# Own buffers for two weight sums, nine low parts of a step on GpSimd, and another order of the up-projection's units

## The reference, cut to what matters

```
up  = rms_norm(x) @ w_up                    # 1024 -> 2 x 2816, 576 tokens
upc = causal_dwconv(up, buf, cw, cb)        # width 3, per feature
val, gate = split(upc)
x   = x + (gelu(gate) * val) @ w_down       # 2816 -> 1024
```

## Time and profile before

| | us |
|---|---|
| median of 3 runs (lowest, highest) | 1084.98 (1084.79, 1086.69) |
| profiled execution, its own time | 1084.38 |
| its span | 1082.2 |
| busy PE, DVE, ACT, POOL | 1023.0, 788.7, 515.6, 425.6 |
| granted TensorE clock, mean | 0.988 |

### The profile page before, as it was taken

The page is one execution under the profiler, slowest core; times in us unless marked ns, Lnnn a source line. Parts: engine busy times, 40 slices in busy tenths (PEclk is TensorE's granted clock), DMA queues, the critical chain, the costliest instruction groups (busy, mean ns, idle before and its releaser), DMA issues.

```text
span 1082.2 us, 19980 instructions
## 1 busy us (share of the span) xinstructions
PE 1023.0 (95%) x7688; PEld 993.2 (92%) x7688; DVE 788.7 (73%) x1280; ACT 515.6 (48%) x935; POOL 425.6 (39%) x276
## 2 busy tenths in 40 slices
PE   8999999999999999999999868889999999999996
PEld 7899999999999999999999867889999999999885
DVE  6786558947576465674545778999999999999954
ACT  7666886223343443433323455544454444445553
POOL 4333443432223222232243425455555545455530
PEclk9999999999999999999999989999999999999998
DMA  8533322666696885946524112333232323223047
GB/s 208 167 101 102 83 79 82 147 191 159 140 259 140 225 215 140 246 110 212 179 80 117 40 39 79 98 92 85 69 105 62 108 70 104 73 76 101 25 101 206
DMA packets 263267, 132.94 MB, mean 123 GB/s; under 512 B 82720, under 2 KB 257045, under 8 KB 262920
## 3 DMA queue, kind: packets, MB, share of 16 engines
q1 hardware_dynamic: 262966, 131.63, 44.6%
q10 hardware_dynamic: 210, 0.07, 0.0%
HBM read 104.17 MB, written 25.29 MB: 120 GB/s over the span
## 4 chain that ended last, share of the span: by engine, by line
PE 57%; DVE 18%; issue 14%; POOL 5%; ACT 3%; DMA 2%; SPq 0%; DVEq 0%; ACTq 0%; POOLq 0%
PE ring L2667 38%; PE bank L3058 4%; PE ring L3072 4%; POOL f_lo L1211 4%; DVE val_taps L1813 3%; DVE f_stage L2398 3%; PE bank L2909 2%; PE ring L3058 2%; POOL wlo L1168 2%; DVE bank L1813 1%; ACT f_hi L1605 1%; DVE f_lo L2479 1%; PE bank L2713 1%; DVE f_stage L2405 1%; DMA d_stage<-in_w_down 1%
## 5 line engine op out<-in xcount | busy, mean ns | idle before, releaser
L1168 POOL TENSOR_TENSOR wlo<-stage,whi 128x1024 fp32r<-128x1024 f32 x78 | 199.0, 2552 | 401.8 <-ACT whi L1224 401.8
L2667 PE MATMUL ring<-x_split,whi 128*128 128x322 f32 (+2 forms) x1952 | 347.5, 300 | 0.0
L2667 PEld LDWEIGHTS ring<-x_split,whi 128*128 128x128 f32 x1952 | 294.4, 189 | 8.9 <-issue 8.1
L1211 POOL TENSOR_TENSOR f_lo<-f_stage,f_hi 128x512 fp32r<-128x512 f32 x110 | 155.1, 1428 | 195.7 <-ACT f_hi L1605 195.6
L2667 PE MATMUL ring<-x_split,wlo 128*128 128x256 f32 (+1 forms) x976 | 210.4, 297 | 0.0
L2667 PEld LDWEIGHTS ring<-x_split,wlo 128*128 128x128 f32 x976 | 164.6, 189 | 0.0
L1224 ACT ACTIVATE whi<-stage 128x1024 fp32r<-128x1024 f32 x79 | 83.3, 1054 | 80.6 <-PE ring L2667 70.6
L1605 ACT ACTIVATE f_hi<-f_stage 128x512 fp32r<-128x512 f32 x154 | 90.4, 627 | 22.8 <-DVE f_stage L2391 11.9
L3058 PE MATMUL bank<-fx_T,f_hi 128*128 128x290 f32 x264 | 79.5, 301 | 8.3 <-ACT sum_two L1688 5.1
L3058 PE MATMUL bank<-fx_T_lo,f_hi 128*128 128x290 f32 x264 | 78.5, 297 | 0.0
L3058 PE MATMUL bank<-fx_T,f_lo 128*128 128x290 f32 x264 | 78.4, 297 | 0.0
(11 more groups left out here) (425 smaller groups left out, 2361.1 us busy)
## 6 DMA issues: line engine op xcount, KB each, us to landing
stage<-in_w_in SPq DMA_DIRECT2D x56, 512.0 KB, 4.2
f_stage<-in_w_up SPq DMA_DIRECT2D x44, 512.0 KB, 5.1
d_stage<-in_w_down SPq DMA_DIRECT2D x40, 256.0 KB, 2.7
stage<-in_w_branch_a SPq DMA_DIRECT2D x8, 512.0 KB, 3.7
c_sample<-in_state_mlstm_C SPq DMA_DIRECT2D x16, 256.0 KB, 6.3
out_s_mlstm_C<-c_sample SPq DMA_DIRECT2D x16, 256.0 KB, 2.4
stage<-in_w_branch_b SPq DMA_DIRECT2D x8, 512.0 KB, 3.8
stage<-in_w_out SPq DMA_DIRECT2D x8, 512.0 KB, 3.7
```

What stands on the lines that cost most here:

```text
L1168: pool.tensor_tensor(spaced(wlo[:, slot]), packed(stage[:, slot, 0:n]), spaced(whi[:, slot]).bitcast(F32), ALU.subtract).then_inc(w_lo, 1)
L1211: pool.tensor_tensor(in_blocks(flo[n % RING], key), packed(piece(key)), in_blocks(fhi[n % RING], key).bitcast(F32), ALU.subtract).then_inc ...
L2667: last = pe.matmul(of(z, t0 or -2, t1), w[:, kk * WS:kk * WS + P], x_, start=kk == 0 and m == 0, stop=kk == kn - 1 and m == 2)
```

## The change

T2 and T4 get one buffer each, `weight_sum_T2` and `weight_sum_T4`, where the SBUF layout had 5888 unused bytes (step 0 keeps the old places). All nine low parts of a step (seven units and two D; seven in a step without D) are GpSimd's. TensorE's order in a step becomes B11, T4', D, T1, B21, T2, D, B22, T3 in place of B11, T1, D, T4', T2, B21, B22, D, T3. VectorE and ScalarE get new orders, and the semaphore counts come from lists of these orders (`sum_order` with C21 of the step before, C11, C22, C12; `weight_sum_order`; `copy_order`; `tap_order`).

```diff
@@ -215,16 +215,16 @@
     for i in range(NPAIR):
         d = down_at(i)
         yield "B11", i
-        yield "T1", i
+        if i:
+            yield "T4", i - 1
         if d:
             yield "D", *d
-        if i:
-            yield "T4", i - 1
+        yield "T1", i
+        yield "B21", i
         yield "T2", i
-        yield "B21", i
-        yield "B22", i
         if d:
             yield "D", d[0], d[1] + 1
+        yield "B22", i
         yield "T3", i
     g0, g1 = GROUPS - 2, GROUPS - 1
     yield "D", g0, 0
@@ -242,8 +242,7 @@
 UNIT = {key: n for n, key in enumerate(PIECES)}
 DOWN = tuple(key for key in PIECES if key[0] == "D")
 DOWN_AT = {key: n for n, key in enumerate(DOWN)}
-QUARTER = {"B11": 0, "B21": 1, "T1": 2, "B22": 3, "T3": 4, "T2": 0, "T4": 1}
-SUM_AT = {"T3": 1, "T1": 2, "T2": 3, "T4": 4}
+QUARTER = {"B11": 0, "B21": 1, "T1": 2, "B22": 3, "T3": 4}
 X_FIRST = {"B11": 1, "T3": 2}
 X_LATER = {"B21": 1, "T1": 2, "T2": 3, "T4": 4, "B22": 5}
 
@@ -268,7 +267,7 @@
     return UNIT[key] + 1
 
 
-SPLIT_BY_DVE = ("B22", "T3")
+SPLIT_BY_DVE = ()
 SPLIT_AT = {key: n + 1 for n, key in enumerate(key for key in PIECES if key[0] not in SPLIT_BY_DVE)}
 SPLIT_AT.update({key: n + 1 for n, key in enumerate(key for key in PIECES if key[0] in SPLIT_BY_DVE)})
 
@@ -288,19 +287,67 @@
     return T_FFN + n
 
 
-def parts(i, n):
-
-    return 3 * i + n
-
-
-def added(i, block):
-
-    return 3 * i + {"C11": 1, "C12": 2, "C22": 3}[block]
-
-
-def scaled(i, block):
-
-    return 4 * i + {"C11": 1, "C12": 2, "C22": 3, "C21": 4}[block]
+def sum_order():
+
+    for i in range(NPAIR + 1):
+        if i:
+            yield "C21", i - 1
+        if i < NPAIR:
+            yield "C11", i
+        if i < NPAIR:
+            yield "C22", i
+        if i < NPAIR:
+            yield "C12", i
+
+
...
+ADDED = numbered(key for key in sum_order() if key[0] != "C21")
+SCALED = numbered(sum_order())
+READY = numbered(key for key in sum_order() if key[0] in ("C21", "C22"))
+WEIGHT_SUM = numbered(weight_sum_order())
@@ -505,7 +552,9 @@
         s_one, s_two, s_five = sb("sum_one", [P, QT], r), sb("sum_two", [P, QT], r + 1184), sb("part_five", [P, QT], r + 2 * 1184)
         r += 3 * 1184
         val_taps = sb("val_taps", [P, CV_N + 4], r)
-        r += 4 * CV_N + 5888
+        r += 4 * CV_N + 32
+        later_sum = {op: sb(f"weight_sum_{op}", [P, QN], r + 4 * QN * n) for n, op in enumerate(("T2", "T4"))}
+        r += 8 * QN + 1760
         dst = [sb(f"d_stage{s}", [P, QN], r + 4 * QN * s) for s in range(2)]
         r += 8 * QN
         x_ops = ("B11", "T3", "B21", "T1", "T2", "T4", "B22")
@@ -540,6 +589,8 @@
 
             if key[0] == "D":
                 return dst[DOWN_AT[key] % 2][:, 0:P * group_size(key[1])]
+            if key[0] in ("T2", "T4"):
+                return later_sum[key[0]][:, :] if key[1] else fst[0][:, ("T2", "T4").index(key[0])]
             return fst[key[1] % 2][:, QUARTER[key[0]]]
 
         def blocks_of(key):
@@ -1049,8 +1100,10 @@
             def load_pair(i):
 
                 if i >= 2:
-                    sp.wait_ge(piece_split, split_done("T4", i - 2))
-                    sp.wait_ge(piece_split_dve, split_done("T3", i - 2))
+                    if i == 2:
+                        sp.wait_ge(piece_split, split_done("T4", 0))
+                    sp.wait_ge(piece_split, split_done("T3", i - 2))
+                    sp.wait_ge(t_done, WEIGHT_SUM["T4", i - 2])
                 for q0, c0 in ((0, P * i), (2, FF + P * i)):
                     sp.dma_start(fst[i % 2][:, q0:q0 + 2].rearrange("p q (k m) -> p (q k) m", m=P),
                                  w_up.rearrange("(k p) m -> p k m", p=P)[:, :, c0:c0 + P]).then_inc(pair_loaded[i % 2], 16)
...
@@ -1717,26 +1771,25 @@
             for i in range(NPAIR):
                 d = down_at(i)
                 part_one(i)
-                ahead("B11", i)
                 if i:
                     first_tap(i - 1, 1)
+                ahead("B11", i)
                 part_five(i)
-                ahead("T1", i)
-                if i:
-                    gelu(i - 1)
-                if d:
-                    ahead("D", *d)
                 if i:
                     ahead("T4", i - 1)
                     first_tap(i - 1, 0)
+                    gelu(i - 1)
                 part_two(i)
+                if d:
+                    ahead("D", *d)
+                ahead("T1", i)
+                ahead("B21", i)
                 ahead("T2", i)
-                ahead("B21", i)
                 if i:
                     product_hi(i - 1)
-                ahead("B22", i)
                 if d:
                     ahead("D", d[0], d[1] + 1)
+                ahead("B22", i)
                 ahead("T3", i)
                 if i:
                     history(i, 0)
@@ -2393,16 +2446,23 @@
             def weight_sum_two(i):
 
                 w = fst[i % 2]
-                dve.wait_ge(t_done, 4 * i + 2)
-                dve.wait_ge(piece_split, split_done("B11", i))
-                tt(w[:, 0], w[:, 2], w[:, 3], ALU.subtract).then_inc(t_done, 1)
+                dve.wait_ge(t_done, WEIGHT_SUM["T1", i])
+                if i == 0:
+                    dve.wait_ge(piece_split, split_done("B11", 0))
+                elif i == 1:
+                    dve.wait_ge(tile_done, T_OUT + 8)
+                else:
+                    dve.wait_ge(piece_split, split_done("T2", i - 1))
+                tt(piece(("T2", i)), w[:, 2], w[:, 3], ALU.subtract).then_inc(t_done, 1)
 
             def weight_sum_four(i):
 
-                w = fst[i % 2]
-                dve.wait_ge(t_done, 4 * i + 3)
-                dve.wait_ge(piece_split, split_done("B21", i))
-                tt(w[:, 1], w[:, 1], w[:, 0], ALU.add).then_inc(t_done, 1)
+                dve.wait_ge(t_done, WEIGHT_SUM["T2", i])
+                if i == 0:
+                    dve.wait_ge(piece_split, split_done("B21", 0))
+                elif i > 1:
+                    dve.wait_ge(piece_split, split_done("T4", i - 1))
+                tt(piece(("T4", i)), fst[i % 2][:, 1], piece(("T2", i)), ALU.add).then_inc(t_done, 1)
 
             def gain(f):
 
...
@@ -2569,43 +2629,36 @@
                 dve.wait_ge(tile_done, unit_done("D", g, m))
                 tt(resid[:, m, META:], of_down(down_out(g, m), META), resid[:, m, META:], ALU.add).then_inc(tile_evicted, 1)
 
+            st.wait()
             for i in range(NPAIR):
-                d, before = down_at(i), down_at(i - 1)
-                if before:
-                    down_evict(before[0], before[1] + 1)
+                d = down_at(i)
                 if i:
-                    sum_two_two(i - 1)
-                else:
-                    st.wait()
-                if i:
+                    other_taps(i - 1, 1)
                     weight_sum_four(i)
-                weight_low("B22", i)
                 if i + 1 < NPAIR:
                     weight_sums(i + 1)
                 if i:
-                    other_taps(i - 1, 1)
-                weight_low("T3", i)
+                    two_one(i - 1)
                 if d:
                     down_evict(*d)
-                if i:
-                    two_one(i - 1)
                 if i + 1 < NPAIR:
                     weight_sum_two(i + 1)
                 if i:
                     other_taps(i - 1, 0)
+                    product(i - 1)
                 sum_one_one(i)
                 if i:
-                    product(i - 1)
+                    product_lo(i - 1)
+                if d:
+                    down_evict(d[0], d[1] + 1)
+                sum_two_two(i)
                 sum_one_two(i)
-                if i:
-                    product_lo(i - 1)
-            i = NPAIR - 1
-            sum_two_two(i)
-            other_taps(i, 1)
-            two_one(i)
-            other_taps(i, 0)
-            product(i)
-            product_lo(i)
+            i = NPAIR
+            other_taps(i - 1, 1)
+            two_one(i - 1)
+            other_taps(i - 1, 0)
+            product(i - 1)
+            product_lo(i - 1)
 
             for m in range(7):
                 down_evict(GROUPS - 1, m)
@@ -3077,17 +3130,16 @@
             for i in range(NPAIR):
                 d = down_at(i)
                 if i >= 2:
-                    pe.wait_ge(sum_scaled, scaled(i - 2, "C21"))
+                    pe.wait_ge(sum_scaled, SCALED["C21", i - 2])
                 up_product("B11", i, True)
                 if i == 0:
                     pe.wait_ge(sq_added, 8)
                     for t0, t1 in halves(M0):
                         last = pe.matmul(of(wide[1], t0, t1), ones[:, :], rbc[:, t0 - M0:t1 - M0], start=True, stop=True)
                     last.then_inc(pe_once, 1)
-                    pe.wait_ge(tile_evicted, T_OUT + 8)
-                else:
-                    pe.wait_ge(sum_scaled, scaled(i - 1, "C12"))
-                up_product("T1", i, True)
+                if i:
```

(27 more changed lines are left out.)

68 lines of the change are left out of this document (50 added, 18 removed).

## The result

The changed kernel takes 1057.89 us (median of 4 runs, 1055.13 to 1061.77) where the kernel before, on the same chip, takes 1085.64: ratio 0.9747, interval 0.971 to 0.9783. Faster by 27.8 and 29.4 us, where 26.2 were forecast.

What follows compares the result with a forecast made beforehand. VectorE was taken to set the pace, TensorE's own D step being 17.75 us against 18.84. Gains of 17.6 + 3.6 + 3.4 + 1.6 = 26.2 us gave 1058.2 to 1058.8, stated as 1059, range 1053 to 1070.

Steps and rivals of the forecast that it cites:

- D steps: Steps 5 to 20, with two down units each: 17.75 us per step, a gain of 16 x 1.10 = 17.6 us.
- short steps 2 to 4: Steps without down units: from 15.5 to 14.3 us each, a gain of 3.6 us, bounds 15.5 and 12 per step.
- start (first and step 1): Steps 0 and 1: second unit of step 2 starts earlier, a gain of 3.4 us, bounds 1 and 5.
- end (step 21 and tail): Second unit of step 21 to its T4: 13.9 instead of 15.45 us, a gain of 1.6, bounds -4 and 3.
- TensorE's own pace: TensorE's work in a D step without the hole before T1, put at 17.75 us and taken as the floor.
- 1.8 us of VectorE room: In a changed D step VectorE finishes 1.8 us early and then waits for T3 at 17.75.
- new wait for ScalarE's first tap: VectorE's gate taps now stand right behind C12, so it waits for ScalarE, about 0.95 us per step.
- The 1.5 charged for waits on GpSimd: In a D step, two VectorE waits on GpSimd's B22 and T3 low parts, 1.5 us together.
- Step 2: Own buffers for T2 and T4: VectorE's waits of 0.49 and 0.81 us for GpSimd go, nothing is copied.
- the charge of "1.5 to 3": In a short step, 1.5 to 3 us of VectorE waits on GpSimd, whose 7 low parts fill 8.75 of it.
- it now outruns the second tap too: In short steps VectorE also waits for ScalarE's second tap, 0.5 us per step.
- moves along: At the end, the chain of D pieces over two stage buffers, some 4.7 us a pair, starts earlier by the same amount.

Runs made afterwards that it cites:

- e1: The changed kernel run once more with no edit: 1056.8 us against 1086.18 for the kernel before, ratio 0.9726.
- e9: The changed kernel with two low parts back on VectorE, B22's behind the gate taps and T3's behind the T2 sum: 1065.71 us, ratio 0.9819.
- e3: The kernel before with only own buffers for T2 and T4, old order and low parts kept: 1067.5 us, ratio 0.9821.
- e4: The kernel before with own buffers and all nine low parts on GpSimd, still in the old order: 1068.76 us, ratio 0.9849.
- e10: The changed kernel with an extra one-column gelu ending ScalarE's start phase, to load gelu's table early: 1053.94 us, ratio 0.9716.
- e8: The changed kernel with ScalarE's copy of the last product ahead of the D pieces' high parts in step 21: 1058.84 us, ratio 0.9762.
- e2: The kernel before with B22's and T3's low parts given to GpSimd and nothing else: 1107.41 us, ratio 1.0195.
- e11: The changed kernel with the T4 sum ahead of the gate taps on VectorE: 1056.08 us, ratio 0.9736.

## Why the prediction was right, and where it was off

Against the table (before minus e1, with the first profiled execution of the changed kernel in brackets):

| term | forecast | measured |
|---|---|---|
| D steps | 17.6 | 18.9 (18.8) |
| short steps 2 to 4 | 3.6 | 7.9 (7.4) |
| start (first and step 1) | 3.4 | 4.5 (2.5) |
| end (step 21 and tail) | 1.6 | -2.5 (-4.3) |
| sum | 26.2 | 28.7 (24.3) |

The sum came within 3 us partly by luck: the short steps gave 4 more than forecast, and the end took 4 to 6 back.

**D steps: right, and TensorE's own pace was the floor as said.** It was put at 17.75, and 17.60 to 17.73 is measured. 1.8 us of VectorE room were forecast and 1.83 is measured. The layout had the low product wait for ScalarE's copy, and so it is: in e9, with two low parts more on VectorE, the low product starts as long before C22 (3.45 us, 3.46 in the changed kernel), and the room is the same 1.83. The new wait for ScalarE's first tap was put at 0.95 and is 0.97. The 1.5 charged for waits on GpSimd were 0.14 in the T4 sum and about 0.4 in the value taps, and a wait of 1.07 for ScalarE's second tap was not in the layout; the room covers both errors. The forecast used all parts of the change for this, and e3 shows that the buffers alone do it. Step 2, "the 0.49 + 0.81 of waits go", was by itself larger than the 1.10 to be won: the sum was there to be made. What the new order adds here is 1.4 us of room (0.4 in e3, 1.8 in e9), which nothing uses.

**Short steps: right in sign, half in size.** The term that was off is the charge of "1.5 to 3" for waits on GpSimd there. A short step of the changed kernel loses about 0.6 that way, in its T4 sum (0.83, 0.15 over) and T2 sum (1.15, 0.47 over). VectorE in one, of the first profile:

```profile
682.72 0.83 DVE L2465 TENSOR_TENSOR weight_sum_T<-f_stage,weight_sum_T 128x512 f32<-128x512 f32 x1
...
685.31 1.15 DVE L2456 TENSOR_TENSOR weight_sum_T<-f_stage 128x512 f32<-128x512 f32 x1
686.38 1.69 DVE L1866 SCALAR_TENSOR_TENSOR val_taps<-up,cols,val_taps 128x592 f32<-128x592 f32 x2
```

GpSimd's burst begins behind the T2 copy, and the value taps, 1.69, are nearly through by then. With 10.9 of work and the 0.97, that is 12.5, and 12.73 is measured. The forecast's reason for the lower end was this very burst; it should have been followed through the step instead of being met half way. The 0.5 for "it now outruns the second tap too" did not occur in these steps.

**Neither order nor low parts alone: both.** With the own buffers in place, steps 2 to 4 take 46.36 (e3), 45.26 with nine low parts (e4), 45.10 with the new order (e9), 38.48 with both (e1). Alone they give 1.1 and 1.3 us, together 7.9. The new order in the old buffers was not run. The forecast counted -1.2 per step for the low parts and added a burst in a better place as a bonus, as if these were separate terms. They are one: the order decides where GpSimd works, the low parts where VectorE does, and only the pair keeps them apart.

**Start.** In range (1 to 5), though "first" also holds what runs ahead of the changed part, and moves by 1.6 us between two executions of the same kernel (648.41 and 646.82). It is also mixed with the clock, as the last section shows: TensorE ran at the lower level for some 6 us behind the wait of 3.1 in the first profile and for some 3 in e1, and not at all there in the kernel before. The wait of 3.1 behind gelu's table load, which the forecast left in, is longer than the 1.4 of before. The row on ScalarE is 1.28 us at 658.81, and e10 moves it to 640.55, off this path.

```profile
658.81 1.28 ACT L1758 ACT_TABLE_LOAD   x1
```

**End: wrong in sign, between its bounds in e1 and just past the lower one in the first profile.** The step said that the chain of D pieces "moves along". It does not: ScalarE's high part waits 1.71 for its load, and the product's copy stands behind it:

```profile
1010.38 0.42 ACT L1658 ACTIVATE f_hi<-d_stage 128x256 fp32r<-128x256 f32 x1 [1.71 <-DMA d_stage<-in_w_down]
1010.71 0.58 ACT L1766 ACTIVATE gh<-bank 128x512 fp32r<-128x512 f32 x1
```

The wait for the low product is 2.7 or 2.8 where 1.3 was the earlier trace rows, and e8 shows that freeing the copy only moves the wait to the pieces. The -4 of the forecast's bounds was for this; the first profile has -4.3, and some 2 of that go with the lower clock there.

**The signs.** C22 distances, the 1.8 before C22, the 0.97 before the gate taps and seven low parts in a row came as listed. The value taps, "near 1.6 for two", take 2.07 or 2.08 in most D steps and 1.7 in short ones; the mean of one is 990 ns, 1668 before. The pair load, forecast just in time, is late in 3 of the 16 D steps, by 0.32 to 0.85, which the room covers.

## What to carry to other kernels

Before an operation is moved to a slower engine, ask which operations of the two exclude each other and where each stands in the step: the same move cost 21 us, was worth nothing, or brought 9 us (e2, e3 to e4, e9 to e1), depending on the buffers and the order around it. A wait that is longer than the gap to the floor is worth removing alone, first. Idle time on an engine off the path is not free space when it is what keeps two engines from meeting (e11).
